# Expert weights loaded as one 8 KB piece per partition instead of two of 4 KB, with the order of the features permuted to match, in a two-layer hybrid attention and mixture-of-experts kernel

## What is computed

```python
D_MODEL, SEQ, CTX_LEN, DEPTH = 1024, 512, 256, 2
N_EXPERTS, EXPERT_FF, EC_CAPACITY = 16, 1024, 2

def modulate(h, shift, scale):
    return h * (1 + scale) + shift

def expert_choice_moe(h, w_router, w_gate, w_up, w_down):
    B, T, D = h.shape
    cap = EC_CAPACITY * T // N_EXPERTS
    aff = jax.nn.softmax((h @ w_router).astype(jnp.float32), axis=-1)
    top_w, top_idx = lax.top_k(aff.transpose(0, 2, 1), cap)
    xg = jax.vmap(lambda hb, ib: hb[ib])(h, top_idx)
    hid = jax.nn.silu(jnp.einsum('becd,edf->becf', xg, w_gate)) * jnp.einsum('becd,edf->becf', xg, w_up)
    ye = jnp.einsum('becf,efd->becd', hid, w_down) * top_w[..., None].astype(h.dtype)
    return jax.vmap(lambda ib, yb: jnp.zeros((T, D), h.dtype).at[ib.reshape(-1)].add(yb.reshape(-1, D)))(top_idx, ye)

...
x = x + mod_l[5] * expert_choice_moe(modulate(rms_norm(x, norm2), mod_l[3], mod_l[4]),
                                     moe_router, moe_w_gate, moe_w_up, moe_w_down)
```

## Time and profile before

| what | value |
|---|---|
| median of three runs | 2678.07 us (2675.78, 2678.07, 2681.22) |
| span of the profiled execution | 2675.0 us |
| the profiled execution's own device time | not listed; the three runs lie 0.8 to 6.2 us above the span |
| busy share of TensorE, VectorE, ScalarE, POOL | 93%, 40%, 25%, 3% |
| bytes moved by the DMA engines | 580.72 MB, 217 GB/s in the mean |
| expert stage of layer 0, about | 938 to 1520 us |
| expert stage of layer 1, about | 2169 to 2665 us |

### The profile page before, as it was taken

How to read it: one execution, slowest core, us unless ns; L and a number is a source line. 1 busy time by engine, 2 the same in 40 slices (tenths; PEclk the granted TensorE clock), 3 DMA queues, 4 the chain that set the end, 5 groups by cost and what they waited for, 6 DMA issues and landing times. The chain is left out here.

```text
span 2675.0 us, 41021 instructions
## 1 busy us (share of the span) xinstructions
PE 2498.9 (93%) x17554; PEld 1572.0 (59%) x17554; DVE 1060.4 (40%) x2329; ACT 675.3 (25%) x1322; POOL 87.6 (3%) x145
## 2 busy tenths in 40 slices
PE   5999999999898899999999889999999889999998
PEld 3888877777676434443444578876676643333432
DVE  4536354344772413213232564546358431111113
ACT  3621232321531212111121353133236210110101
POOL 1000100000000000000100000100000000000000
PEclk9999999999998899999999999999999999999999
DMA  6111565255630699897989312232216279999997
GB/s 214 56 48 33 161 200 176 87 168 176 221 138 10 267 351 395 304 393 303 380 338 363 125 40 64 61 98 75 67 60 194 92 289 409 409 409 409 409 409 281
DMA packets 241828, 580.72 MB, mean 217 GB/s; under 512 B 11462, under 2 KB 120240, under 8 KB 240624
## 3 DMA queue, kind: packets, MB, share of 16 engines
q1 hardware_dynamic: 232160, 550.21, 55.3%
q0 software_dynamic: 9488, 27.90, 3.2%
HBM read 554.94 MB, written 23.13 MB: 216 GB/s over the span
## 5 line engine op out<-in xcount | busy, mean ns | idle before, releaser
L971 PE MATMUL ps<-h_hi,m_lo 128*128 128x512 f32 (+1 forms) x1152 | 345.3, 371 | 1.7 <-DVE arena L2137 1.7
L1387 PE MATMUL ps<-arena 128*32 128x512 f32 x1740 | 259.2, 593 | 1.6 <-ACT arena L1811 1.1
L1388 PE MATMUL ps<-arena 128*32 128x512 f32 x588 | 258.0, 593 | 0.0
L944 PE MATMUL ps<-m_lo,h_hi 128*128 128x256 f32 (+1 forms) x1248 | 235.2, 290 | 9.0 <-DVE m_lo L2110 7.0
L971 PEld LDWEIGHTS ps<-h_hi,m_lo 128*128 128x128 f32 x1152 | 207.6, 189 | 53.6 <-issue 17.0
L944 PEld LDWEIGHTS ps<-m_lo,h_hi 128*128 128x128 f32 x1248 | 197.8, 196 | 17.7 <-issue 13.7
L971 PE MATMUL ps<-h_lo,m_lo 128*128 128x512 f32 (+1 forms) x576 | 204.8, 356 | 0.0
L1533 PE MATMUL ps<-arena 128*64 128x512 f32 x832 | 187.8, 597 | 10.7 <-DMA arena<-in_moe_w_up 8.0
L944 PE MATMUL ps<-m_lo,h_lo 128*128 128x256 f32 (+1 forms) x624 | 178.0, 285 | 0.0
L1387 PEld LDWEIGHTS ps<-arena 128*32 128x32 f32 x1740 | 70.4, 110 | 164.2 <-issue 160.7
L944 PE MATMUL ps<-h_hi,m_lo 128*128 128x512 f32 (+1 forms) x512 | 143.1, 357 | 10.2 <-DVE h_lo L2215 9.4
(11 more groups left out here) (398 smaller groups left out, 4511.7 us busy)
## 6 DMA issues: line engine op xcount, KB each, us to landing
arena<-in_moe_w_up SPq DMA_DIRECT2D x101, 1024.0 KB, 13.3
arena<-in_moe_w_gate SPq DMA_DIRECT2D x100, 1024.0 KB, 11.4
arena<-in_moe_w_down SPq DMA_DIRECT2D x100, 1024.0 KB, 12.9
ring<-in_w_in SPq DMA_DIRECT2D x42, 1024.0 KB, 5.5
arena<-in_ada_w SPq DMA_DIRECT2D x40, 1024.0 KB, 5.5
oT<-in_moe_w_up SPq DMA_DIRECT2D x27, 1024.0 KB, 11.5
oT<-in_moe_w_down SPq DMA_DIRECT2D x24, 1024.0 KB, 9.1
oT<-in_moe_w_gate SPq DMA_DIRECT2D x16, 1024.0 KB, 9.7
```

Of the source, the lines that this page charges most:

```text
L944: last = mm(to, stationary, moving, start=at == 0 and k == 0, stop=at == 2 and k == KD - 1)
L971: last = mm(to, w[:, k, cols], h[:, k, seg], start=n == 0 and k == 0, stop=n == 2 and k == KD - 1)
L1387: mm(ps[r][32 * b:32 * b + 32, :], c_xg[:, k, j, 32 * b:32 * b + 32], w, start=k == 0, stop=k == KD - 1)
L1388: last = mm(ps[r][96:128, :], c_xg[:, k, j, 32 * r:32 * r + 32], up[:, kk, 512:1024], start=k == 0, stop=k == KD - 1)
```

## The change

The rows of a weight piece are dealt to partitions in pairs: partition p now gets rows 2 p and 2 p + 1 of the 256, one run of 8 KB. So a feature tile k no longer holds 128 neighbouring features but every second one of 256, and all that is contracted with the weights is put in the same order: the router's rows, the transposes of xn2 (L1028, L1034), of gathered rows (L1454) and of hidden rows (L1433, L1565), the gather's stationary slices (L1576), and the columns of shift and scale (L900, half of L1045's vectors). The stride of two stands in the stationary operand each time. The gate columns and the output of the down product keep the natural order.

```diff
+PAIRED_AT = (128, 192)
...
+        def pair_columns(k):
+
+            return slice(2 * P * (k // 2) + k % 2, 2 * P * (k // 2) + 2 * P, 2)
+
+        def turned_columns(h, c):
+
+            return slice(c, 2 * P, 2) if 24 <= 2 * (h % 24) < 40 else tile(c)
...
                     src = a["moe_w_" + matrix][l, bass.ds(g * GE + j, 1), kp * 256:kp * 256 + 256, :]
-                    sp.dma_start(raw_pair(l, g, i), src.rearrange("e (k p) n -> p (e k) n", p=P)
+                    sp.dma_start(raw_pair(l, g, i), src.rearrange("e (p k) n -> p (e k) n", p=P)
                                  ).then_inc(pair_in[n % SLOTS_OF[l]], 16)
...
-                pool.dma_start(router[:, 0:KD, :], a["moe_router"][l].rearrange("(k p) e -> p k e", p=P)
+                pool.dma_start(router[:, 0:KD, :].rearrange("p (a b) e -> p a b e", b=2), a["moe_router"][l].rearrange("(a p b) e -> p a b e", b=2, p=P)
                                ).then_inc(small_in, 16)
...
-                            last = tr(ada_bank(h)[:, 256 + P * c:256 + P * c + ADA_ROWS], ada_row[0:ADA_ROWS, tile(c)], ident[0:ADA_ROWS, 0:ADA_ROWS])
+                            last = tr(ada_bank(h)[:, 256 + P * c:256 + P * c + ADA_ROWS], ada_row[0:ADA_ROWS, turned_columns(h, c)], ident[0:ADA_ROWS, 0:ADA_ROWS])
...
-                        last = tr(ps[2 + k % 2][:, tile(t - CT)], xn2[:, t, tile(k)], ident)
+                        last = tr(ps[2 + k % 2][:, tile(t - CT)], xn2[:, t, pair_columns(k)], ident)
...
-                            last = tr(ps[4 + k % 2][:, tile(t)], xn2[:, t, tile(k)], ident)
+                            last = tr(ps[4 + k % 2][:, tile(t)], xn2[:, t, pair_columns(k)], ident)
...
-                tr(ps[1][:, 0:R_ALL], vecs[0:R_ALL, :], ident[0:R_ALL, 0:R_ALL]).then_inc(vecs_up, 1)
+                tr(ps[1][:, 0:R_ALL], vecs[0:R_ALL, :], ident[0:R_ALL, 0:R_ALL])
+                for b in range(2):
+                    for half in range(2):
+                        last = mm(ps[1][64 * half:64 * half + 64, PAIRED_AT[b]:PAIRED_AT[b] + R_ALL // 2], vecs[0:R_ALL, b:P:2],
+                                  ident[0:R_ALL, half:R_ALL:2], start=True, stop=True)
+                last.then_inc(vecs_up, 1)
...
-                            last = tr(ps[4 + b][:, k * ROWS:(k + 1) * ROWS], rows[:, tile(k)], ident[0:ROWS, 0:ROWS])
+                            last = tr(ps[4 + b][:, k * ROWS:(k + 1) * ROWS], rows[:, pair_columns(k)], ident[0:ROWS, 0:ROWS])
...
-                        last = tr(ps[dt % gather_banks(g)][:, tile(p)], g_rows[p][:, tile(dt)], ident)
+                        last = tr(ps[dt % gather_banks(g)][:, tile(p)], g_rows[p][:, pair_columns(dt)], ident)
...
-                        last = tr(ps[4][:, k * CAPL:(k + 1) * CAPL], hid[0:CAPL, tile(k)], ident[0:CAPL, 0:CAPL])
+                        last = tr(ps[4][:, k * CAPL:(k + 1) * CAPL], hid[0:CAPL, pair_columns(k)], ident[0:CAPL, 0:CAPL])
...
-                        last = mm(bank[:, 0:GE * CAPL], xn2[:, CT + t, tile(dt)],
+                        last = mm(bank[:, 0:GE * CAPL], xn2[:, CT + t, pair_columns(dt)],
...
-                v.tensor_copy(vT[:, :], ps[1][:, 0:R_ALL]).then_inc(vecs_ok, 1)
+                for r in (slice(0, R_AB + 24), slice(R_AB + 40, R_N2), slice(R_N2 + 8, R_ALL)):
+                    v.tensor_copy(vT[:, r], ps[1][:, r])
+                for r, n in ((R_AB + 24, 16), (R_N2, 8)):
+                    for b in range(2):
+                        at = PAIRED_AT[b] + r // 2
+                        last = v.tensor_copy(vT[:, r + b:r + n:2], ps[1][:, at:at + n // 2])
+                last.then_inc(vecs_ok, 1)
```

## The result

The changed kernel has a median of 2688.25 us against 2678.07 us, a ratio of 1.0034 with a 95% interval of 1.0023 to 1.0045. The prediction said 2673.3 us, with a range of 2669 to 2682. The profiled execution's span is 2687.8 us, 12.8 us above that of before; the timed difference is 9 to 10 us, and the five executions of a kernel scatter by 5 to 7 us, so the trace is read stretch by stretch here and not by its total.

The account below looks back on a forecast made before the run. TensorE is busy 93% of the span, but loads just pace layer 1's two whole expert turns. Saving 5.5 us of load waits and adding 0.7 for vector copies gives - 4.8: 2678.07 to 2673.3 us, range 2669 to 2682.

Parts of the forecast that it names:

- the price of the moved part: Strided stationary operands on TensorE in transposes and gather: put at nothing, between bounds of nothing and doubling 138 to 140 ns.
- the row that is nearest: 16 products of 512 moving f32 columns in 3.65 us: 9.0 B per ns, against 7.3 for a strided weight load.
- The rival that I gave 0.17: Strided weight loads lengthen 432 transposes in both layers, making the kernel slower; decides from 11 ns per transpose; chance 0.17.
- a third longer: Case of the slower rival: 46 ns more per transpose, + 20 us, 2693 us if the loads' gain is kept.
- The loads' gain: Layer 1's expert stage: 8 KB packets raise the rate 2.0% to 417 GB/s, saving 5.5 us of TensorE's load waits.
- the same formula: Saving in layer 1's expert stage for rate gain g: the smaller of 305 g and 58 g + 4.3 us.
- the two whole turns: Layer 1's expert stage, four experts each, 2261.13 to 2507.83 us: 122.7 and 124.0 us, forecast to fall to 121 to 121.5.
- if turns stay at 123 us with a faster stream: Sign that the forecast is wrong, read in layer 1's expert stage; the forecast was turns of 121 to 121.5 us.
- The rival in which the rate stays at 409: Layer 1's loads: 409 GB/s is a full queue's limit, not the packet's; 2678.8 us; chance 0.20.
- The vectors' part: Start of layer 1: seven small VectorE copies replace one ahead of the first projection, + 0.7 us, bounds + 0.2 and + 1.0.
- The gather's 256 loads at no cost: Layer 1's gather (L1576): 256 weight loads with a stride of two, forecast to stay at 190 ns.
- the 9216-byte stretch: Spilled gates read in 9216-byte packets, two clean microseconds at 419 GB/s; used for the rate's upper end, 424.

Follow-up runs that it names:

- the strides alone: The changed kernel with the loads of before (two pieces of 4 KB), strides, router order and vector columns kept: 2688.56 us, ratio 1.0046 to the kernel before.
- the loads alone: The kernel before with only the 8 KB loads put in, contracting features in mismatched order: 2669.46 us against 2677.72, ratio 0.9972.

## Why the prediction was wrong

**What failed.** It is one step, the price of the moved part: "I take nothing, by the row that is nearest". The row compared a stationary operand with a moving one, two paths of TensorE that need not read alike, and bytes spanned per ns said nothing about either. The row also says less than I took from it. Gate and up run side by side, and their products start in pairs, as the timeline shows where it lists them one by one:

```profile
2200.43 0.59 PE L1533 MATMUL ps<-x_sb,arena 128*64 128x512 f32 x1
2200.44 0.59 PE L1533 MATMUL ps<-oT,arena 128*64 128x512 f32 x1
2200.86 0.59 PE L1533 MATMUL ps<-x_sb,arena 128*64 128x512 f32 x1
```

So one of the two streams reads 2048 B in 0.43 us, 4.8 B per ns, less than the 7.3 that the row was to vouch for.

The price is 42 ns for a transpose of layer 0's hidden rows, 57 ns in layer 1, and 16 to 18 ns where 128 rows are turned. The rival that I gave 0.17 was the one that came: it decides from 11 ns per transpose on, and 256 of the 432 pay four to five times that. Both ends stood in the text (nothing, and a doubling of 140 ns); the measured weight load of 209 to 216 ns is half of the way. The middle (70 ns for 432 transposes, 30 us, about 2703 us) would have missed by as much as the end did, 15 us, on the other side. With no row between ends that far apart, the rival should have had a larger chance and the range its whole width.

**What the rival had wrong.** It took a load's extra time for the transpose's: the loads are longer by 69 to 75 ns, the work by 16 to 57 ns, since the pace of the products had covered a part, all but 11 ns of it where 128 rows are turned. It priced a third longer at 20 us; half longer came to 9 us net. Of 432 transposes the 128 of layer 1's experts (6.4 us with fast loads) are paid from what the loads gave back. Layer 0's expert stage (5.8 us) has no cover, as the rival said, and no loads to gain from. Another 1 to 2 us lie with the norm's transposes (0.8 us from start to start over both layers) and the modulation's. The single traces scatter by more than that: ahead of the two stages lie 923.8 and 645.3 us before the change, 927.7 and 647.0 after it, and 923.7 and 643.8 with the strides alone. And the 1.7 us at layer 0's gate and up products can't be laid to the strides.

**What held.** The loads' gain: I took 417 GB/s from 409 and 419 (421 came), so 5.5 us; by the same formula 421 gives 58 x 0.029 + 4.3 = 6.0, and the loads alone gave 6.8 us in the stage. The rate came out higher than the line through 2 and 4 KB had it (415), because the 2 KB row was three microseconds at 397 GB/s; the full stream of 2 KB packets runs at 386, and the line through 386 and 409 gives 422. The waits on loads left in layer 1's stage are 2.1 us (3.2 with the loads alone), as forecast (3). With the loads alone the two whole turns take 120.8 and 120.7 us, close to the 121 that TensorE was to need; in the changed kernel they take 122.7 and 122.6, and the 1.9 us more are 32 transposes at 57 ns. So one of the signs of being wrong came, "if turns stay at 123 us with a faster stream", and it came from the strides. The rival in which the rate stays at 409 is out. The vectors' part: 0.7 us forecast; between L1045 and the first projection of layer 1 there are now 8.75 us (1535.27 to 1544.02) in place of 8.36 (1523.88 to 1532.24), 0.4 us. Seven copies take 0.63 us in place of 0.24:

```profile
1538.16 0.35 DVE L2514 COPY vT<-ps 128x24 f32<-128x24 f32 x3
...
1538.42 0.37 DVE L2518 COPY vT<-ps 128x8 f32<-128x8 f32 x4
1538.83 0.26 DVE L2204 TENSOR_TENSOR modT<-modT,vT 128x96 f32<-128x96 f32 x1
```

The gather's 256 loads at no cost: right, for another reason than mine; their extra 7 ns lie beside the products.

**Two slips without weight.** A doubling was put at 2739 us without the loads' gain, a third at 2693 with it; with it the doubling is 2734. And the upper end of the rate, 424 GB/s, took the 9216-byte stretch to be at a DMA share of 1; its share was 0.99, which gives some 427.

**What the sum does.** Loads alone - 0.28%, strides alone + 0.46%, both + 0.34%. The first two would add up to + 0.18%. What is missing in the single runs is 3.0 us (6.4 - 3.4) of stride price that slow loads hide, 0.11%. The remaining 0.05% is inside the intervals.

## What to carry to other kernels

A layout that makes a load's pieces longer is worth what the stage where loads are waited for can take, here 7 us in one of two layers. It may have to be paid for on every path that reads the new order, so apply it only to the layer that waits. Put the stride where it is free. Here that was the elementwise operation ahead of the transposes, not the stationary operand; with it, layer 1's share of the change alone made the kernel faster by 0.20%. Before a strided operand is costed at nothing, look for a row that reads that same operand with a stride, and if there is none, treat the price as open.

## What the runs showed of the hardware

- A transpose's weight load of 128 f32 columns takes 138 to 141 ns with neighbouring columns, whether they begin at an even or an odd one, and 192 to 218 ns at strides of 2, 3, 4, 7 and 8, with no growth from 2 on.
- With a stride of two, transposes of 64, 96 and 128 rows start 120 ns apart within a group; without one, 62, 83 and 109 ns. The fewer rows are turned, the more the stride costs.
- A plain f32 product's weight load of 128 columns takes 190, 197, 329 and 337 ns at strides of 1, 2, 4 and 8. Why the two kinds differ stays open; no run here tells.
- VectorE's two-operand product on 512 columns from SBUF and PSUM (687 ns) and its scaling of 1024 columns in SBUF (0.75 us) take the same time with a stride of two in what they read.
- A full stream of 2, 4 and 8 KB packets runs at 386, 409 and 421 GB/s, which makes 84.9, 160.2 and 311.3 ns for a packet on one of 16 engines. At 4 KB it is the same whether a partition's two rows are neighbours or 128 rows apart.
